# One pair of a diffusion block on TensorE: operands at one offset within 512 bytes, and another order of the last pair's fillers

## The chip, the cores and the metric

The kernel runs on one core of a Trainium2 chip. Its time is device microseconds of one execution; the number for a kernel is the median of several. TensorE does the matrix products; VectorE, ScalarE and GpSimd read and write SBUF next to it; SyncE and the other engines issue DMAs.

## The reference, cut to what matters

Two layers over 1024 latent tokens and 256 context tokens of width 1024, all in float32. The even layer projects to eight groups of 1024 channels (B, C, X, G for a gated convolution; Q, K, V, BG for neighbourhood attention of 16 heads plus the context keys), and an output projection of 2048 channels back to 1024. The odd layer is a bidirectional RG-LRU.

```python
z = u_lat @ w_in                                   # even: 1024 -> 8192
y_a = z_B * dwconv(z_C * z_X, w_conv) * silu(z_G)
y_b = neighbourhood_attention(q, k, v, k_c, v_c, rpb) * silu(z_BG)
h = h + gate * (concatenate([y_a, y_b]) @ w_out)   # 2048 -> 1024
z = u_lat @ w_in_o                                 # odd: 1024 -> 4096
x = dwconv(z[..., :2048]) + b
r, i = sigmoid(blockdiag(x, w_ra)), sigmoid(blockdiag(x, w_ri))
a = exp(8 * r * log_sigmoid(lam)); b = sqrt(1 - a*a) * i * x
y = (scan_forward(a, b) + scan_backward(a, b)) * silu(z[..., 2048:])
out = rmsnorm(h + gate * (y @ w_out_o))
```

## The kernel before

Every product is split in two parts for accuracy: an operand is kept as `hi` (rounded to the product's format) and `lo` (the rest), and each product runs three times: hi x hi, hi x lo, lo x hi. ScalarE makes `hi`, VectorE or GpSimd makes `lo`.

The even layer works in eight pairs of heads (`PAIRS`). A pair has 20 steps, one for each tile of 128 queries of a head: steps 0 to 15 have 640 keys (latent tiles), steps 16 to 19 have 256 (context tiles). In a step TensorE issues the scores of step s+1, the transposes of step s (`turn`), then filler (a projection unit of the pair, 24 products of 512 or 256 columns), then `weigh` (probabilities times V). VectorE does `row_max(s+1)`, `turn_lo(s)`, `normalise(s+1)`, then what filler asks of it, then `output(s)`. ScalarE does `turn_hi(s)`, `exp(s+1)`, the filler's copies, `copy_low(s)`.

In the last pair (`last`) there is no next pair's Q, K, V to project. `LAST_UNITS` says which units of C, X, B, G a step takes; from step 9 on, `OUT_CHUNKS` gives each step (tile, first chunk, last chunk) of the out projection's first pass: tile t is 128 tokens, its product has 16 chunks (`YC`) of 128 channels, three products of 512 columns each. What isn't done there is done in `projection()`, from tile `OUT_BEGUN` on. The weights and y have to be split first: `out_w_hi/lo(r)` for chunks 2r and 2r+1, `out_y_hi/lo(q, b, half)` for eight chunks of tile q. They are put into the steps by three functions on ScalarE and VectorE: `within(s)` is before the units' work, `ahead(s)` behind it, and `behind(s)` after `copy_low` or `output`. A second pass (`out_run`, L1652 on TensorE) does the other 512 output columns with `w1hi`, `w1lo`.

The odd layer has eight blocks, each with units X1, Z0, Z1, X0 (L2322) and four gate groups (L2341) on TensorE; then the final projection (L2351). Weight halves there are `whi` and `wlo`, of three slots; ScalarE's queue order is the order of `body`.

Buffers are laid out by hand by `Map`: the address of a tensor is `BASE` plus what stood before it; `align()` rounds up to 128 bytes.

Of the kernel before, what the change touches and what calls it, by code (L numbers as in the profile page):

```python
# [21 lines left out]
ALU = mybir.AluOpType  # L22
# [3 lines left out]
P = 128  # L26
# [11 lines left out]
YC = 16  # L38
# [40 lines left out]

class Map:  # L80
# [8 lines left out]
    def align(self):  # L89
        self.at = (self.at + P - 1) // P * P  # L90
# [77 lines left out]
LAST_UNITS = ((0,), (1,), (2, 3), (4,), (5, 6), (7, 8), (9,), (10,), (11,))  # L168


OUT_CHUNKS = {9: (0, 0, 5), 10: (0, 5, 11), 11: (0, 11, YC), 12: (1, 0, 5), 13: (1, 5, 11), 14: (1, 11, YC),
              15: (2, 0, 5), 16: (2, 5, 9), 17: (2, 9, 13), 18: (2, 13, YC), 19: (3, 0, 4)}
OUT_BEGUN = 4


def even_layer(nc, a, out, sem, k, ps, dram, uhi, ulo, ctx):
# [24 lines left out]
    m.align()  # L201
    prob_at = Map.BASE + m.at
    prob = m("probs", [P, 2, KEYS])
    pt = m("probs_t", [P, KEYS // P, 2 * P], F32R)
    low, t2 = m("pv_low", [P, 2 * P]), m("pv_out", [P, P])
    negmax, sums, rcp = m("neg_max", [P, 2]), m("row_sums", [P, 2]), m("row_rcp", [P, 2])
    small, th = m("c_cols", [P, KC, 2]), m("c_tanh", [P, KC, 2])
    ss, rms, rinv = m("sum_squares", [P, NT]), m("rms", [P, NT]), m("rms_inverse", [P, NT])
# [48 lines left out]
    ut, xn = om("u_tile", [P, KC, P]), om("xn_tile", [P, D])  # L257
# [164 lines left out]
    with nc.Block() as block:  # L422
        @block.sync
        def _(sp):
# [144 lines left out]
            def projection():  # L569
# [32 lines left out]
                load_x(0, 4, 0)  # L602
# [76 lines left out]
        def _(act):  # L679
# [232 lines left out]

            def within(s):

                if s == 7:
# [1615 lines left out]
```

## Time and profile before

| | us |
|---|---|
| median of 3 runs | 2328.14 (2328.09 to 2329.01) |
| the profiled execution | 2327.99 |
| its span | 2326.2 |
| TensorE busy in it | 2254.2 |

The span is the time from the first to the last instruction. The rows below were read from its profile. L-numbers are lines of the kernel; a name such as `ps<-u_hi,w_hi` is the tile written and the tiles read; `x24` is a count. "Idle before" is the time for which the engine stood before an instruction, and behind the arrow is who released it. A matmul's duration contains the filling and draining of the array, so products overlap: the time that one costs is the distance from its start to the next one's.

### The profile page before, as it was taken

Reading aid. Unit: us, or ns where it says so; the run is one execution under the profiler, and the core shown is the slowest. Engines: PE = TensorE matmul, PEld = TensorE weight load, DVE = VectorE, ACT = ScalarE, POOL = GpSimd, SP = SyncE. Lnnn points to the kernel's source line nnn. Section 1 sums busy time; section 2 is a strip of 40 time slices with the busy share of each in tenths; the row PEclk is TensorE's granted clock in tenths of the full one; section 3 lists DMA queues with packets and bytes.
Section 4 is the critical chain, followed back from the end, with each engine's and each line's share of the span. In section 5 each row is a group of like instructions: output and inputs, shape, how many; then the busy total and the mean of one; then the engine's idle time right before and its main releaser. Section 6 shows DMA issues by size and latency. Waiting matters only on the chain. (4 is left out here: it accounts for less than half of the span.)

```text
span 2326.2 us, 33502 instructions
## 1 busy us (share of the span) xinstructions
PE 2254.2 (97%) x11996; PEld 1910.1 (82%) x11996; DVE 1505.7 (65%) x2407; ACT 1168.1 (50%) x1696; POOL 493.5 (21%) x287
## 2 busy tenths in 40 slices
PE   6999999999999999999998999799999999999998
PEld 4788888888888888888886788688888888887787
DVE  4576575765757657577567536648667766776765
ACT  4534444345344453444434244347876787678311
POOL 0232231322323323233221030022222222220000
PEclk9999999999999999999998999899999999999999
DMA  7111221111112111122223756201111111113521
GB/s 292 37 54 52 66 61 66 54 52 62 54 59 72 52 57 59 34 70 70 66 63 121 214 168 180 85 31 55 56 54 55 55 46 64 55 55 127 208 82 64
DMA packets 146665, 187.50 MB, mean 81 GB/s; under 512 B 50520, under 2 KB 109144, under 8 KB 143448
## 3 DMA queue, kind: packets, MB, share of 16 engines
q1 hardware_dynamic: 138888, 166.67, 22.7%
q10 hardware_dynamic: 7632, 18.88, 2.2%
q8 instruction: 94, 1.54, 0.3%
q14 instruction: 51, 0.42, 0.1%
HBM read 155.62 MB, written 29.88 MB: 80 GB/s over the span
## 5 line engine op out<-in xcount | busy, mean ns | idle before, releaser
L1390 PE MATMUL ps<-u_hi,w_hi 128*128 128x512 f32 (+1 forms) x1464 | 533.2, 364 | 0.0
L1390 PE MATMUL ps<-u_hi,w_lo 128*128 128x512 f32 (+1 forms) x1464 | 519.9, 355 | 0.0
L1390 PE MATMUL ps<-u_lo,w_hi 128*128 128x512 f32 (+1 forms) x1464 | 517.8, 354 | 0.0
L1390 PEld LDWEIGHTS ps<-u_hi,w_lo 128*128 128x128 f32 x1464 | 276.4, 189 | 40.1
L1390 PEld LDWEIGHTS ps<-u_lo,w_hi 128*128 128x128 f32 x1464 | 277.1, 189 | 35.2
L1390 PEld LDWEIGHTS ps<-u_hi,w_hi 128*128 128x128 f32 x1464 | 276.5, 189 | 35.2
L2322 PE MATMUL ps<-u_hi,o_w_hi 128*128 128x512 f32 (+1 forms) x640 | 240.0, 375 | 9.4 <-POOL o_w_lo L1897 9.4
L732 ACT ACTIVATE probs<-probs,neg_max 128x640 f32<-128x640 f32 (+1 forms) x160 | 122.7, 767 | 248.5 <-DVE neg_max L1062 248.5
L1897 POOL TENSOR_TENSOR o_w_lo<-o_w_raw,o_w_hi 128x1024 fp32r<-128x1024 f32 x48 | 143.0, 2979 | 466.7 <-ACT o_w_hi L1916 466.7
L2322 PE MATMUL ps<-u_hi,o_w_lo 128*128 128x512 f32 (+1 forms) x640 | 238.7, 373 | 0.0
L2322 PE MATMUL ps<-u_lo,o_w_hi 128*128 128x512 f32 (+1 forms) x640 | 238.3, 372 | 0.0
L640 POOL TENSOR_TENSOR bias_tile<-bias_piece,col_mask 128x384 f32<-128x384 f32 x128 | 141.1, 1106 | 451.0 <-DVE neg_max L1062 450.9
L621 POOL TENSOR_TENSOR w_lo<-w_stage,w_hi 128x1024 fp32r<-128x1024 f32 x61 | 146.1, 2396 | 402.6 <-ACT w_hi L685 402.6
L1081 DVE TENSOR_TENSOR pv_low<-ps,pv_low 64x256 f32<-64x256 f32 x160 | 66.6, 416 | 237.7 <-ACT pv_low L743 236.3
L738 ACT ACTIVATE probs_t<-ps 128x640 fp32r<-128x640 f32 (+1 forms) x160 | 102.7, 642 | 105.6 <-PE ps L1414 101.8
L2322 PEld LDWEIGHTS ps<-u_hi,o_w_hi 128*128 128x128 f32 x640 | 120.8, 189 | 31.6 <-POOL o_w_lo L1897 9.8
L2322 PEld LDWEIGHTS ps<-u_hi,o_w_lo 128*128 128x128 f32 x640 | 120.8, 189 | 23.6
L2322 PEld LDWEIGHTS ps<-u_lo,o_w_hi 128*128 128x128 f32 x640 | 120.9, 189 | 22.1 <-issue 0.2
L2341 PE MATMUL ps<-x_hi,o_w_hi 128*128 128x512 f32 (+1 forms) x384 | 136.7, 356 | 1.4 <-ACT lru_r L1962 1.4
L2341 PE MATMUL ps<-x_hi,o_w_lo 128*128 128x512 f32 (+1 forms) x384 | 137.3, 358 | 0.0
L2341 PE MATMUL ps<-x_lo,o_w_hi 128*128 128x512 f32 (+1 forms) x384 | 136.9, 357 | 0.0
L1074 DVE TENSOR_TENSOR probs_t<-ps,probs_t 128x640 fp32r<-128x640 f32 (+1 forms) x160 | 118.3, 739 | 18.5 <-ACT probs_t L738 18.3
(247 smaller groups left out, 4612.8 us busy)
## 6 DMA issues: line engine op xcount, KB each, us to landing
w_stage<-in_w_even SPq DMA_DIRECT2D x63, 512.0 KB, 3.8
o_w_raw<-in_w_odd SPq DMA_DIRECT2D x48, 512.0 KB, 3.7
ada_piece<-in_w_ada SPq DMA_DIRECT2D x20, 1024.0 KB, 5.9
y_raw<-y_scratch SPq DMA_DIRECT2D x40, 512.0 KB, 6.2
wout_raw<-in_w_out SPq DMA_DIRECT2D x16, 512.0 KB, 5.9
y_scratch<-h_backward SPq DMA_DIRECT2D x16, 512.0 KB, 3.0
final_w_raw<-in_w_out SPq DMA_DIRECT2D x8, 1024.0 KB, 11.4
final_y_raw<-y_scratch SPq DMA_DIRECT2D x15, 512.0 KB, 4.6
```

What stands on the lines that cost most here:

```text
L621: nc.gpsimd.tensor_tensor(wlo[:, slot, :], stage[:, slot, :], whi[:, slot, :].bitcast(F32), ALU.subtract).then_inc(w_lo, 1)
L640: nc.gpsimd.tensor_tensor(dst, src, col, ALU.add).then_inc(t_ready, 1)
L732: nc.scalar.activation(prob[:, b, q], prob[:, b, q], ACT.Exp, scale=-1.0, bias=negmax[:, b:b + 1], accum_out=sums[:, b:b + 1]).then_inc(ex ...
L738: nc.scalar.activation(pt[:, 0:n, 0:P], turned_bank(n), ACT.Copy).then_inc(pt_hi, 1)
L1074: nc.vector.tensor_tensor(pt[:, 0:n, P:2 * P], turned_bank(n), pt[:, 0:n, 0:P].bitcast(F32), ALU.subtract).then_inc(pt_lo, 1)
L1081: nc.vector.tensor_tensor(low[r, :], ps[0:64, 6, 0:2 * P], low[r, :], ALU.add).then_inc(pv_used, 1)
L1390: last = nc.tensor.matmul(ps[:, bank(j, g), 0:t - f], w[:, slot, c * P:(c + 1) * P], x[:, c, f:t], start=(c == 0 and n == 0), stop=(c == K ...
L1897: nc.gpsimd.tensor_tensor(wlo[:, slot, :], wraw[:, slot, :], whi[:, slot, :].bitcast(F32), ALU.subtract).then_inc(w_lo, 1)
L2322: last = nc.tensor.matmul(ps[:, bank(j, g), 0:t - f], w[:, slot, c * P:(c + 1) * P], x[:, c, f:t], start=(c == 0 and q == 0), stop=(c == K ...
L2341: last = nc.tensor.matmul(ps[:, 2 + 3 * mat + g, 0:q1 - q0], w[:, slot, at:at + P], x[:, c, q0:q1], start=(c == 0 and q == 0), stop=(c == ...
```

## The change

It has two parts. First, `align()` rounds up to 512 bytes instead of 128, `ODD_RAW` is rounded down to a multiple of 512, and the x buffers of the odd layer get 1408 columns instead of 1312 (a multiple of 512 bytes); small tensors move into the gaps so made, or over others, to fit. Second, the last pair: units 9 and 10 are split in halves over steps 6 to 9, the out projection of tiles 0 and 1 is spread over steps 11 to 19 (before: of four tiles over 9 to 19), the weight and y splits are spread with it, `gate_diagonal` goes from VectorE to ScalarE and the gate rows from steps 12 and 16 to 16 and 18. In the odd layer ScalarE's `split_hi(n, GW0)` moves from the end of a block to behind `evacuate(n, X1, 1)`.

```diff
+LINE = 512
...
-        self.at = (self.at + P - 1) // P * P
+        self.at = (self.at + LINE - 1) // LINE * LINE
...
-ODD_RAW = Map.TOP - Map.BASE - 3 * KC * P * 4
+ODD_RAW = (Map.TOP - Map.BASE) // LINE * LINE - 3 * KC * P * 4
...
-LAST_UNITS = ((0,), (1,), (2, 3), (4,), (5, 6), (7, 8), (9,), (10,), (11,))
-
-
-OUT_CHUNKS = {9: (0, 0, 5), 10: (0, 5, 11), 11: (0, 11, YC), 12: (1, 0, 5), 13: (1, 5, 11), 14: (1, 11, YC),
-              15: (2, 0, 5), 16: (2, 5, 9), 17: (2, 9, 13), 18: (2, 13, YC), 19: (3, 0, 4)}
-OUT_BEGUN = 4
+LAST_UNITS = (((0, 0, 8),), ((1, 0, 8),), ((2, 0, 8), (3, 0, 8)), ((4, 0, 8),), ((5, 0, 8), (6, 0, 8)), ((7, 0, 8),),
+              ((8, 0, 8), (9, 0, 4)), ((9, 4, 8),), ((10, 0, 4),), ((10, 4, 8),), ((11, 0, 8),))
+
+
+OUT_CHUNKS = {11: (0, 0, 4), 12: (0, 4, 8), 13: (0, 8, 12), 14: (0, 12, YC), 15: (1, 0, 4), 16: (1, 4, 7), 17: (1, 7, 10),
+              18: (1, 10, 13), 19: (1, 13, YC)}
+OUT_BEGUN = 2
...
+    row_at = ada_at + 4 * 512 * 4
+    ut = over("u_tile", [P, KC, P], row_at)
+    grow = over("gate_rows", [P, 2, 2, 512], row_at + 2 * 512 * 4)
+    diag = over("gate_diag", [P, 2, 512], row_at + 6 * 512 * 4)
+    ones = over("gate_ones", [P, P], row_at + 8 * 512 * 4)
+    assert row_at + 8 * 512 * 4 + P * 4 <= x_at
...
-            return [(*ORDER[u], 0, KC) for u in LAST_UNITS[s]] if s < len(LAST_UNITS) else []
+            return [(*ORDER[u], c0, c1) for u, c0, c1 in LAST_UNITS[s]] if s < len(LAST_UNITS) else []
...
-                for t in (2, 3):
-                    for half in range(2):
-                        load_y(t, t, half)
+                for half in range(2):
+                    load_y(2, 2, half)
+                store_rest(LAT // 2, LAT, LAT_STEPS)
+                for half in range(2):
+                    load_y(3, 3, half)
                 load_x(0, 2, 0)
-                store_rest(LAT // 2, LAT, LAT_STEPS)
-                load_x(0, 3, 1)
-                sp.wait_ge(yb_stored[1], 16 * i + 16)
-                for half in range(2):
-                    load_y(4, 4, half)
                 store_rest(LAT, TOK, STEPS)
                 for stored in yb_stored:
                     sp.wait_ge(stored, 16 * PAIRS + (16 if stored is yb_stored[1] else 0))
+                for half in range(2):
+                    load_y(4, 4, half)
+                load_x(0, 3, 1)
...
+            def gate_diagonal(pass_, s):
+
+                for c in range(4):
+                    ins = nc.scalar.activation(diag[:, s, c * P:(c + 1) * P], k["ident"][:], ACT.Copy,
+                                               scale=k["modx"][:, 4 * pass_ + c, s:s + 1])
+                ins.then_inc(diag_done, 1)
+
             def within(s):
 
+                if s == 12:
+                    out_w_hi(4)
+                elif s == 13:
+                    out_w_hi(6)
+                elif s == 14:
+                    out_w_hi(7)
+
+            def ahead(s):
+
+                if s == 10:
+                    out_y_hi(0, 0, 0)
+
+            def behind(s):
+
+                i = PAIRS - 1
                 if s == 7:
-                    out_w_hi(0)
-                    out_w_hi(1)
-                elif s == 8:
-                    out_w_hi(2)
-                elif s == 9:
-                    out_w_hi(4)
-                elif s == 10:
-                    out_y_hi(0, 0, 1)
-                    out_w_hi(6)
-                elif s == 12:
-                    out_y_hi(1, 1, 1)
-
-            def ahead(s):
-
-                if s == 8:
-                    out_y_hi(0, 0, 0)
-
-            def behind(s):
-
-                i = PAIRS - 1
-                if s == 6:
                     act.wait_ge(ya_done, i + 1)
                     store_conv(act, i, 0, LAT // 2)
                 elif s == 8:
-                    out_w_hi(3)
+                    out_w_hi(0)
+                elif s == 9:
+                    out_w_hi(1)
+                elif s == 10:
+                    out_w_hi(2)
                     act.wait_ge(ya_done, i + 3)
                     store_conv(act, i, LAT // 2, LAT)
                     store_conv(act, i, LAT, TOK)
-                elif s == 9:
+                elif s == 11:
+                    out_w_hi(3)
+                    out_y_hi(0, 0, 1)
+                elif s == 12:
                     out_w_hi(5)
-                elif s == 10:
-                    out_w_hi(7)
-                elif s == 11:
+                elif s == 13:
+                    act.wait_ge(ya_stored, 32 * PAIRS + 16)
+                    gate_diagonal(0, 0)
+                elif s == 14:
                     out_y_hi(1, 1, 0)
-                elif s == 12:
+                    gate_diagonal(0, 1)
+                elif s == 15:
+                    out_y_hi(1, 1, 1)
+                elif s == 16:
                     copy_gate_row(0)
-                elif s == 13:
                     out_y_hi(2, 0, 0)
-                elif s == 14:
+                elif s == 17:
                     out_y_hi(2, 0, 1)
-                elif s == 15:
+                elif s == 18:
+                    copy_gate_row(1)
                     store_half(0)
-                elif s == 16:
-                    copy_gate_row(1)
-                    out_y_hi(3, 1, 0)
-                elif s == 17:
-                    out_y_hi(3, 1, 1)
-                    store_half(1)
...
-                for t in range(2, NT):
+                for t in range(1, NT):
                     for half in range(2):
                         out_y_hi(t + 2, t % 2, half)
                     store_half(t)
+                    if t == 3:
+                        act.wait_ge(row_mm, 2)
+                        for v in range(2):
+                            gate_diagonal(1, v)
...
             def within(s):
 
-                if s == 7:
+                if s == 12:
+                    out_w_lo(4)
+                elif s == 13:
+                    out_w_lo(6)
+                elif s == 14:
+                    out_w_lo(7)
+
+            def ahead(s):
+
+                if s == 10:
+                    out_y_lo(0, 0, 0)
+
+            def behind(s):
+
+                if s == 8:
                     out_w_lo(0)
+                elif s == 9:
                     out_w_lo(1)
-                elif s == 8:
+                elif s == 10:
                     out_w_lo(2)
-                elif s == 9:
-                    out_w_lo(4)
-                elif s == 10:
+                elif s == 11:
+                    out_w_lo(3)
                     out_y_lo(0, 0, 1)
-                    out_w_lo(6)
                 elif s == 12:
+                    out_w_lo(5)
+                elif s == 14:
+                    out_y_lo(1, 1, 0)
+                elif s == 15:
                     out_y_lo(1, 1, 1)
-                elif s == 14:
+                elif s == 16:
+                    out_y_lo(2, 0, 0)
+                elif s == 17:
+                    out_y_lo(2, 0, 1)
                     first_half(0, half_link)
-                elif s == 16:
-                    first_half(1, half_link)
-
-            def ahead(s):
-
-                if s == 8:
-                    out_y_lo(0, 0, 0)
-
-            def behind(s):
-
-                if s == 8:
-                    out_w_lo(3)
-                elif s == 9:
-                    out_w_lo(5)
-                elif s == 10:
-                    out_w_lo(7)
-                elif s == 11:
-                    out_y_lo(1, 1, 0)
-                    dve.wait_ge(ya_stored, 32 * PAIRS + 16)
-                    gate_diagonal(0, 0).then_inc(diag_done, 1)
-                elif s == 13:
-                    out_y_lo(2, 0, 0)
-                elif s == 14:
-                    out_y_lo(2, 0, 1)
-                elif s == 15:
-                    gate_diagonal(0, 1).then_inc(diag_done, 1)
-                elif s == 16:
-                    out_y_lo(3, 1, 0)
-                elif s == 17:
-                    out_y_lo(3, 1, 1)
...
-                for t in range(2, NT):
+                for t in range(1, NT):
                     first_half(t, half_link)
                     for half in range(2):
                         out_y_lo(t + 2, t % 2, half)
-                    if t == 2:
-                        dve.wait_ge(row_mm, 2)
-                        gate_diagonal(1, 0)
-                        gate_diagonal(1, 1).then_inc(diag_done, 1)
...
-                    if last and s == 12:
-                        pe.wait_ge(row_done, PAIRS)
-                        gate_row(0)
                     if last and s == 16:
                         pe.wait_ge(mod_copied, PAIRS)
+                        gate_row(0)
+                    if last and s == 18:
+                        pe.wait_ge(grow_done, 1)
                         gate_row(1)
                     if s == 14:
-                        if last:
-                            pe.wait_ge(grow_done, 1)
...
-                pe.wait_ge(diag_done, 3)
+                pe.wait_ge(diag_done, 4)
...
-                out_products(OUT_BEGUN - 1, OUT_CHUNKS[STEPS - 1][2], YC)
...
-XCOLS = 1312
+XCOLS = 1408
...
+    gaps = [X_AT + (q * XCOLS + QCOLS + 4) * 4 for q in range(3)]
+    m.at = gaps[0]
+    convw, convb, lam = m("conv_w4", [P, 64]), m("conv_b4", [P, 16]), m("lam", [P, 32])
...
-                split_hi(0, GW0)
 
             def body(n, last):
-                for g in range(1, NG):
-                    evacuate(n, X1, g)
+                evacuate(n, X1, 1)
+                split_hi(n, GW0)
+                evacuate(n, X1, 2)
...
-                    split_hi(n + 1, GW0)
```

## Rows read from the trace of the kernel before

**Rows 1.** The page, busy time of each engine, and the granted clock in 40 slices (9 is full).
```profile
PE 2254.2 (97%) x11996; PEld 1910.1 (82%) x11996; DVE 1505.7 (65%) x2407; ACT 1168.1 (50%) x1696; POOL 493.5 (21%) x287
...
PEclk9999999999999999999998999899999999999999
```

**Rows 2.** Waits of TensorE: us in total, times, longest.
```profile
PE ps L2322 <- POOL o_w_lo L1897: 9.4, 1, 9.4
PE ps L1424 <- DVE probs_t L1074: 7.2, 10, 2.3
```

**Rows 3.** Groups of instructions by form, TensorE: busy us, mean ns, idle before.
```profile
L2322 PE MATMUL ps<-u_hi,o_w_lo 128*128 128x512 f32 x512 | 202.6, 396 | 0.0
...
L1652 PE MATMUL ps<-wout_hi,u_hi 128*128 128x512 f32 x80 | 31.9, 399 | 0.0
```

**Rows 4.** The chain that ended last: start, us, what; one odd block, last stage.
```profile
1605.20 25.17 PE ps L2322 x120
1630.36 6.97 PE ps L2341 x36
...
1649.87 5.56 PE ps L2322 x24
...
1662.40 14.00 PE ps L2322 x72
...
2166.88 151.28 PE ps L2351 x666
```

**Rows 5.** Timeline of TensorE: start, us, line; two runs of products, first and next.
```profile
844.80 0.39 PE L1390 MATMUL ps<-u_hi,w_hi 128*128 128x512 f32 x1
...
850.25 0.28 PE L1406 MATMUL ps<-k_stack,q_stack 128*128 128x256 f32 x1
...
1372.02 0.40 PE L1652 MATMUL ps<-wout_hi,u_hi 128*128 128x512 f32 x1
...
1383.21 0.40 PE L1652 MATMUL ps<-wout_hi,y_hi 128*128 128x512 f32 x1
```

**Rows 6.** Windows: us, busy (instructions) of PE, PEld, DVE, ACT, POOL, granted clock, DMA.
```profile
1226.80:1233.60 6.80, 4.58 (x14) 3.44 (x14) 6.70 (x12) 3.40 (x6) 0.41 (x2) 0.50 0.84 291
1257.60:1260.90 3.30, 3.30 (x9) 2.57 (x8) 2.81 (x7) 1.88 (x3) 1.24 (x2) 0.50 0.54 159
```

**Rows 7.** Timeline of TensorE, last pair, steps 7, 10 to 12 and 19.
```profile
1212.35 0.38 PE L1414 MATMUL ps<-ident,probs 128*128 128x128 f32 x2
...
1242.83 0.50 PE L1637 MATMUL ps<-u_hi 128*128 128x512 f32 x1 [3.39 <-DVE u_lo L1150]
...
1252.86 0.77 PE L1424 MATMUL ps<-probs_t,v_stack 128*128 128x256 f32 x5
...
1254.05 0.71 PE L1414 MATMUL ps<-ident,probs 128*128 128x128 f32 x5
...
1296.54 0.41 PE L1424 MATMUL ps<-probs_t,v_stack 128*128 128x256 f32 x2
```

**Rows 8.** Timeline of VectorE, last pair, steps 7 and 10 to 12.
```profile
1222.01 0.69 DVE L1029 SCALAR_TENSOR_TENSOR conv_out<-conv_c,conv_out 128x512 f32<-128x512 f32 x1
...
1248.64 1.21 DVE L1144 TENSOR_TENSOR u_lo<-wout_raw,u_hi 128x1024 fp32r<-128x1024 f32 x1
1249.78 0.81 DVE L1062 CUSTOM_DVE_ANT_0 probs<-ps,bias_tile 128x640 f32<-128x640 f32 x1
...
1250.52 0.81 DVE L1074 TENSOR_TENSOR probs_t<-ps,probs_t 128x640 fp32r<-128x640 f32 x1
...
1251.79 0.55 DVE L1069 TENSOR_SCALAR probs<-probs,row_rcp 128x640 f32<-128x640 f32 x1
1254.08 0.42 DVE L1081 TENSOR_TENSOR pv_low<-ps,pv_low 64x256 f32<-64x256 f32 x1 [1.73 <-ACT pv_low L743]
```

**Rows 9.** Timeline of SyncE's queue and of ScalarE: load of the out weights, first split.
```profile
1211.34 2.59 SPq L522 DMA_DIRECT2D wout_raw<-in_w_out  x4
...
1217.92 2.01 ACT L889 ACTIVATE u_hi<-wout_raw 128x1024 fp32r<-128x1024 f32 x2 [1.62 <-DMA wout_raw<-in_w_out]
```

More of the change, by code:

```diff
@@ L200, in even_layer @@
     convw = m("conv_w", [P, 24])
-    m.align()
+    m.at = (m.at + P - 1) // P * P
     prob_at = Map.BASE + m.at
@@ L204, in even_layer @@
     pt = m("probs_t", [P, KEYS // P, 2 * P], F32R)
+    low_at = m.at
+    small, th = m("c_cols", [P, KC, 2]), m("c_tanh", [P, KC, 2])
+    ss, rms, rinv = m("sum_squares", [P, NT]), m("rms", [P, NT]), m("rms_inverse", [P, NT])
+    m.at = low_at
     low, t2 = m("pv_low", [P, 2 * P]), m("pv_out", [P, P])
     negmax, sums, rcp = m("neg_max", [P, 2]), m("row_sums", [P, 2]), m("row_rcp", [P, 2])
-    small, th = m("c_cols", [P, KC, 2]), m("c_tanh", [P, KC, 2])
-    ss, rms, rinv = m("sum_squares", [P, NT]), m("rms", [P, NT]), m("rms_inverse", [P, NT])
     assert Map.BASE + m.at <= Map.TOP - 2 * KC * P * 4 - SILU_BYTES
@@ L1151, in out_y_lo @@
                                         y_half(0, b, half).bitcast(F32), ALU.subtract).then_inc(y_lo, 1)
-            def gate_diagonal(pass_, s):
-                for c in range(4):
-                    ins = nc.vector.tensor_scalar(diag[:, s, c * P:(c + 1) * P], k["ident"][:],
-                                                  k["modx"][:, 4 * pass_ + c, s:s + 1], None, ALU.mult)
-                return ins
             def first_half(t, link):
@@ L1198, in behind @@
                 if s == 8:
+                    out_w_lo(0)
+                elif s == 9:
+                    out_w_lo(1)
+                elif s == 10:
+                    out_w_lo(2)
+                elif s == 11:
                     out_w_lo(3)
-                elif s == 9:
+                    out_y_lo(0, 0, 1)
+                elif s == 12:
                     out_w_lo(5)
-                elif s == 10:
-                    out_w_lo(7)
-                elif s == 11:
+                elif s == 14:
                     out_y_lo(1, 1, 0)
-                    dve.wait_ge(ya_stored, 32 * PAIRS + 16)
-                    gate_diagonal(0, 0).then_inc(diag_done, 1)
-                elif s == 13:
+                elif s == 15:
+                    out_y_lo(1, 1, 1)
+                elif s == 16:
                     out_y_lo(2, 0, 0)
-                elif s == 14:
+                elif s == 17:
                     out_y_lo(2, 0, 1)
-                elif s == 15:
-                    gate_diagonal(0, 1).then_inc(diag_done, 1)
-                elif s == 16:
-                    out_y_lo(3, 1, 0)
-                elif s == 17:
-                    out_y_lo(3, 1, 1)
+                    first_half(0, half_link)
             def out_a(pass_, t, b, i):
@@ L1690, in odd_layer @@
     m = Map(nc, PHASE)
-    convw, convb = m("conv_w4", [P, 64]), m("conv_b4", [P, 16])
-    grow, ones = m("final_gate_row", [P, D]), m("final_ones", [P, P])
-    lru, lam = m("lru_columns", [P, 5, 32]), m("lam", [P, 32])
+    grow, lru = m("final_gate_row", [P, D]), m("lru_columns", [P, 5, 32])
     bri, bra, L, Lh, nLh = (lru[:, q, :] for q in range(5))
-    own = m("lru_block_columns", [P, 5, 2, 2])
-    e_, z_, z2, den, low = (m(x, [P, 32]) for x in ("log_e", "log_z", "log_z2", "log_den", "log_low"))
     ss, var = m("final_ss", [P, NLT, 2]), m("final_var", [P, NLT])
@@ L1712, in odd_layer @@
     H0_AT = m.at
-    H0, H1 = m("h_forward", [P, 2, QCOLS]), m("h_backward", [P, 2, QCOLS])
+    H0 = m("h_forward", [P, 2, QCOLS])
+    H1_AT = m.at
+    H1 = m("h_backward", [P, 2, QCOLS])
     sg = m("silu_gate", [P, 2, LAT])
@@ L1717, in odd_layer @@
     wlo = m("o_w_lo", [P, 3, KC * P], F32R)
+    gaps = [X_AT + (q * XCOLS + QCOLS + 4) * 4 for q in range(3)]
+    m.at = gaps[0]
+    convw, convb, lam = m("conv_w4", [P, 64]), m("conv_b4", [P, 16]), m("lam", [P, 32])
+    assert m.at <= X_AT + XCOLS * 4
+    m.at = gaps[1]
+    own = m("lru_block_columns", [P, 5, 2, 2])
+    e_, z_, z2 = (m(x, [P, 32]) for x in ("log_e", "log_z", "log_z2"))
+    assert m.at <= X_AT + 2 * XCOLS * 4
+    m.at = gaps[2]
+    den, low = (m(x, [P, 32]) for x in ("log_den", "log_low"))
+    assert m.at <= X_END
     def over(name, shape, at, dt=F32):
@@ L1739, in odd_layer @@
     junk = over("final_squares", [P, 512], D * 4)
-    diag = over("final_diag", [P, KC * P], H0_AT)
+    diag, ones = over("final_diag", [P, KC * P], H0_AT), over("final_ones", [P, P], H1_AT)
     def y_raw(q):
```

18 lines of the change are left out of this document (4 added, 14 removed).

## The prediction

> **What bounds the kernel now.** I read the busy table and the slices first: TensorE is busy in 97% of the span, at its upper clock (2.4 GHz) in nearly all slices [rows 1]. The waits of TensorE come next: the two longest groups after the start are 9.4 us at the seam into the odd layer and 7.2 us in ten waits of L1424 for VectorE's `turn_lo` [rows 2]; the waits of L1637 in the last pair stand in the timeline [rows 7]. So almost every microsecond is either a matmul's period or one of few holes, and the change touches both: the periods of the odd layer and of the out projection's second pass, and the holes of the last pair.
>
> Third, the period. The chain of waits merges back-to-back matmuls, so its lines give it. One block of the odd layer repeats: 120 products of L2322 in 25.17 us, 36 of L2341 in 6.97, 24 of L2322 in 5.56, 72 in 14.00; the last stage runs 666 products of L2351 in 151.28, so 227.1 ns each [rows 4]. A 24-unit with 512 columns in 5.56 us is 231.7 ns each. The even layer, by the timeline, does 24 from 844.80 to 850.25, 227.1 ns; L1652 does 48 from 1372.02 to 1383.21, 233.1 ns [rows 5]. All are 512 columns, and the windows and slices put them all at the upper clock.
>
> I then worked out each operand's offset within 512 bytes of `Map.BASE` from the allocations. L1390 (`whi`, `wlo`, `uhi`, `ulo`): all 0; L1637: all 0; L2351: all 0. These run at 227. L1652: y at 0, `w1hi/w1lo` at 128. L2322: `whi`, `uhi`, `ulo` at 0, `wlo` at 352. L2341: `xhi` at 128 and 256, `xlo` at 384 and 0, `wlo` at 352. These run at 230 to 233. Three places alike, three unlike, no exception.
>
> **Part 1, alignment** (`LINE`, `ODD_RAW`, `XCOLS`, `align`). Price of each term if the unlike ones take 227.1 ns:
> L2322. With 512 columns: 24 x 0.2271 = 5.45 instead of 5.56, gain 0.11. The 120-line has four such units and one of 256 columns: 25.17 - 4 x 5.56 = 2.93 for the latter, which I leave; gain 0.44. The 72-line: 0.22. A block: 0.44 + 0.22 + 2 x 0.11 = 0.88 us. Eight blocks less the last one's X0 plus the prologue's X0: 7.0. I take off 0.5 for the products after each change of shape, which could need a few periods to settle. 6.5 us.
> L2341. 36 in 6.97: 24 of 512 and 12 of 260 columns. 24 x 0.2271 = 5.45 leaves 1.52 for the twelve, 127 ns each, more than the 2.93/24 = 122 ns of 256 columns; at 124 ns the line would be 6.94. Gain 0.03 of each of 32 lines, 1.0 us; bounds 0 (its 512 runs are only 12 long, too short to settle) and 2.5.
> L1652. 48 x (0.2331 - 0.2271) = 0.29 a tile, ten tiles, 2.9; less the same settling, 2.5 us.
> Sum 10.0 us, bounds 0 (the offset isn't the cause) and 12.5. All lies on the path: TensorE has no hole in the second pass and in the odd blocks. The counts agree with the list of groups: L2322 has three operand pairs of 512 products with 512 columns each, L1652 six of 80 [rows 3]. The seam's 9.4 us stays: `split_lo` and the load before it are not touched. ScalarE's `split_hi(n, GW0)` is moved back by an `evacuate` within its own queue; its user is 5 units (25 us) later, and the `evacuate` of g1 that it stood ahead of comes 1.05 us earlier: nothing either way, bound +-0.5.
>
> At this place the Trainium skill speaks against the change: "TensorE: Matmul & The Clock Gate", Part 2, step-by-step, has two independent read ports for the streaming and the stationary operand, so that loading the next weights takes no read bandwidth from the running matmul. By it the two addresses could not matter and part 1 is worth 0. The trace doesn't agree in its plain form: periods differ by 3% between stages at one clock [rows 4, 5].
>
> **Part 2, the last pair.** Before, steps 5 to 19 run with this pattern. In step 11 nothing is late [rows 7, 8]: products, `weigh` at 1252.86, next `turn` at 1254.05 (1.19 later), `output` on VectorE at 1254.08 (1.22 later), about 1.0 us with its two narrower operations; a split there takes 1.15 start to start; `row_max` at 1249.78, `turn_lo` ends 1251.33 (+1.55), normalised at 1252.34 (+2.56). Two units' gate products on VectorE cost 2 x 0.70. A chunk of out products is 3 x 0.227 = 0.68; from `turn` to its first filler I take 0.46 (its row's 0.71 less the drain of the last transpose, an estimate). Two rules follow: `weigh(s)` starts no sooner than `row_max(s+1)` + 1.6, and `turn(s+1)` no sooner than + 2.63.
> Now I place the new steps with them. Steps up to 5 lose a 256-column unit (2.9 us) and step 6 takes it: `turn(7)` at 1209.6 instead of 1212.35 [rows 7]. Then VectorE is what is late. It runs `row_max(s+1)`, `turn_lo`, normalise (2.56), the step's splits, `output` 1.0. Weigh of step 8: 1217.65; `out_w_hi(0)` then waits for its DMA: before, issue 1211.34 to ready 1217.92 [rows 9], 6.6 us; now issued at 1213.1, ready 1219.7, VectorE 1.1 late. Steps 9 and 10 carry G1 (1.4) + w1, and G2 (0.8) + y + w2: `weigh` at 1223.8 and 1229.95, with holes of 1.8 and 1.6. Steps 11 and 12, two splits each: `weigh` 1236.65 and 1243.35, holes 1.9 and 2.7 (chunk 6 of step 12 also waits for `out_w_lo(3)`, behind step 11). Step 13: 1249.45, hole 1.7 (`out_w_lo(5)`). Step 14 asks for chunks 12 to 15, and chunk 14 needs `out_w_lo(7)`, which stands inside step 14 itself behind `row_max(15)`, `turn_lo`, normalise: ready at `row_max(15)` (1252.8) + 2.56 + 0.3 for ScalarE's half + 1.15 = 1256.8, wanted at 1253.2 (two chunks behind `out_w_lo(6)`), a hole of 3.5. `weigh(14)` 1258.1, (15) 1264.3 after waiting for `out_y_lo(1,1,0)`, (16) 1268.7, (17) 1273.3, (18) 1278.6, (19) 1281.9.
> Before, `weigh(19)` starts at 1296.54 [rows 7] with 52 chunks of out products done; now 32. The 20 missing ones cost 20 x 0.68 = 13.6 us in `projection`. 1296.5 - 1281.9 - 13.6 = 1.0 us gained. Against it the clock: before, TensorE's granted clock is at 0.50 (1.2 GHz) in 1226.8 to 1233.6 and in two shorter stretches, of which one stands here [rows 6]; one follows the 3.39 us hole at 1242.83 [rows 7]; they are inside the old times. The new 3.5 us hole should bring one of the short ones: half of 3.3 us, 1.6. So part 2 is +0.6 us. Bounds: all holes gone, -10 (the walk's twelve holes, about 20 us, less what VectorE needs anyway); slow clock through steps 9 to 18, +12 (below).
> What follows is hidden: tile 2's y (splits of steps 16 and 17) is ready, tile 3's has 10.9 us (a tile: 48 x 0.227), tile 4's loads are issued after `store_rest`, about 4 us into tile 2, and needed 17 us later. `gate_diagonal` goes from VectorE to ScalarE, where eight 128-column copies meet an engine 50% busy; nothing waits but `gate_row`, two steps on. The overlaid scratch tiles cost no time.
>
> **Sum.** Profiled run 2327.99 (span 2326.2), 0.15 below the median of the runs shown. -10.0 + 0.6 = -9.4; from the median 2318.7. I say 2318.5.
>
> **Rivals.**
> A, the last pair comes out better than walked. VectorE and ScalarE queues slip past each other and the twelve holes shrink by half: 8 us of the 20, 2310.5. For it: before, ten `turn_lo` waits cost only 7.2 us in the whole run [rows 2]. Against: every step from 9 to 12 has 2.4 us or more of splits on top of 3.5 us of attention, against 4.5 us of TensorE work.
> B, the offset is not the cause (what the skill's rule says): part 1 is 0, the time is 2328.7 (2328.1 + 0.6), no change. For it: in L2322 only one operand in three pairs is unlike, and yet the whole 24-unit is slow; the odd layer could be slow through ScalarE's and VectorE's traffic. Against: L1652 is slow in a stage whose other engines do much the same as in L1637's.
> C, slower than before: the holes of steps 9 to 14 come so thick that the clock stays at 1.2 GHz from step 9 to 18. There 9 products start in 3.3 us [rows 6], where 14 fit at 0.227. TensorE's own work in steps 9 to 18 (1.75 us of attention in steps 9 to 15, about 0.8 in 16 to 18, 12 or 9 products, 24 of 256 columns and an ada row in step 10, two gate rows) is about 42 us at the upper clock, 84 at the lower; the walk gives these steps 62 us. So the full case costs 22 us: 2328.1 - 10 - 1 + 22 = 2339. It decides, that is eats part 1, from half the stretch on (11 us, 2328); three quarters, 2334, is what I name as its time. For it: five holes of 1.6 to 1.9 us and two above 2.5 in a row, where before a 3.39 us hole was enough for a drop. Against: a hole of 1.8 us between products at full rate is less idle than any that a drop followed.
> If only L1652 and half of L2322 speed up the time is 2323, within the forecast's range.
>
> **How the numbers follow.** Forecast 0.62, own range 2313 to 2324; A 0.16, B 0.13, C 0.09. Range 2308 to 2327: leaves out C, half of B, and A's far end. The measurement tells 0.2% (4.7 us) from no change: faster is the forecast, A, and a bit of B with A's steps: 0.81. Within 0.2%: most of B and weak forms of the forecast, 0.11. Slower: C with part 1 small, and B with drops: 0.08.
>
> **What would show it.** The 24-lines of L2322 at 5.46 and its 120-line near 24.7; L1652's 48 in 10.9; L2341's 36 near 6.94. A wait of L1637 for `out_w_lo(7)` of 2.2 to 3.5 us in step 14; short waits of L1424 for `turn_lo` in most of steps 8 to 18. `weigh(19)` near 1282, out pass 1 beginning within 3 us of before. Wrong is the forecast if L2322's lines stay at 5.56, or if clock 0.5 covers more than 10 us of the last pair.

## The result, and the profile after

The kernel after takes 2333.51 us (median of 12 runs, 2332.19 to 2335.17) against 2328.47 us before (12 runs, 2327.37 to 2329.48): 1.0024 of the time before, 95% interval 1.0016 to 1.0033. It is 5 us slower, and the forecast was 10 us faster, outside its range. The profiled execution took 2335.17 us, its span is 2333.4 (2326.2 before): 7.2 us to explain in the two traces.

Busy table and granted clock of the kernel after, as in [rows 1]:
```profile
PE 2247.4 (96%) x11996; PEld 1907.0 (82%) x11996; DVE 1524.5 (65%) x2391; ACT 1172.3 (50%) x1712; POOL 487.3 (21%) x287
...
PEclk9999999999999999999999999899999999999999
```
TensorE is busy for 6.8 us less and yet the kernel is longer. VectorE has fewer instructions and is busy for 18.8 us more. Its instructions got longer; that is the row to keep in mind.

The chain of waits of the kernel after answers to [rows 4]: start, us, what, and how many products. Three lines of a block, and the last stage:
```profile
1526.72 24.67 PE ps L2326 x120
1551.39 6.90 PE ps L2345 x36
1558.28 5.48 PE ps L2326 x24
...
2174.03 151.28 PE ps L2355 x666
```
L2326 is L2322 of before, L2345 is L2341. 120 products take 24.67 us instead of 25.17, 36 take 6.90 instead of 6.97, 24 take 5.48 instead of 5.56. The second pass of the output projection, as in [rows 5]; these two products are 48 apart, in 10.88 us instead of 11.19:
```profile
1374.39 0.39 PE L1646 MATMUL ps<-wout_hi,u_hi 128*128 128x512 f32 x1
...
1385.27 0.39 PE L1646 MATMUL ps<-wout_hi,y_hi 128*128 128x512 f32 x1
```
So the products are as quick as forecast. From the same timelines I cut the span at four places (start of the out projection's second pass, which is pass 1 in the code, first product of L2326, first product of the last stage, end). Everything up to pass 1 is 2.4 us longer (1374.39 against 1372.02), pass 1 and the tail up to the odd layer 2.5 us shorter (134.39 against 136.92), the odd layer 7.3 us longer (638.47 against 631.13), the last stage equal (186.1). Sum +7.2.

The waits of TensorE, as in [rows 2], show two groups that before doesn't have among its longest, with L2345 and with the conv_in of L2326:
```profile
PE ps L1420 <- DVE probs_t L1091: 11.1, 14, 1.8
PE ps L2326 <- POOL o_w_lo L1902: 9.4, 1, 9.4
PE ps L2345 <- DVE x_lo L2121: 6.7, 7, 1.2
...
PE ps L2326 <- ACT conv_in L1930: 4.0, 7, 0.6
```
Seven waits each: one in every block but one. A block, from one `columns_of` on VectorE to the next, takes 79.4 us instead of 78.2, and within it TensorE stands for 1.5 us (0.9 and 0.6, the two groups above) where it stood for 0.0. A block of the same products without a hole takes 77.05 us (e8 below), so the holes, with the overlap of products that is lost at each, cost 2.3 us a block, more than the 1.1 that the quicker products saved.

Where it comes from shows on VectorE and GpSimd in one stretch of the same block, behind the gate products of p = 3. First before: VectorE's `lru_root`, the `lru_b` that uses it, the long scan and the next block's `x_lo`, and GpSimd's `split_lo` of the next block's Z0 and GW0 weights (start, us, engine, line):
```profile
1845.37 1.50 DVE L2137 SCALAR_TENSOR_TENSOR lru_root<-lru_root,lru_r 128x1284 f32<-128x1284 f32 x1
1848.22 2.27 DVE L2142 SCALAR_TENSOR_TENSOR lru_b<-lru_b,lru_root 128x1284 f32<-128x1284 f32 x1 [1.35 <-ACT lru_root L1977]
...
1851.25 4.31 DVE L2151 TENSOR_TENSOR_SCAN h_backward<-lru_a,h_backward,lru_b 128x1024 f32<-128x1024 f32 x1
...
1861.54 3.01 DVE L2117 TENSOR_TENSOR x_lo<-x_conv,x_hi 128x1284 fp32r<-128x1284 f32 x2
...
1845.50 3.63 POOL L1897 TENSOR_TENSOR o_w_lo<-o_w_raw,o_w_hi 128x1024 fp32r<-128x1024 f32 x1 [9.89 <-ACT o_w_hi L1916]
1850.85 2.56 POOL L1897 TENSOR_TENSOR o_w_lo<-o_w_raw,o_w_hi 128x1024 fp32r<-128x1024 f32 x1 [1.72 <-ACT o_w_hi L1916]
```
The same after, and the first operation of the next block's convolution:
```profile
1848.01 3.57 DVE L2141 SCALAR_TENSOR_TENSOR lru_root<-lru_root,lru_r 128x1284 f32<-128x1284 f32 x1
1852.93 1.50 DVE L2146 SCALAR_TENSOR_TENSOR lru_b<-lru_b,lru_root 128x1284 f32<-128x1284 f32 x1 [1.34 <-ACT lru_root L1982]
...
1855.19 2.35 DVE L2155 TENSOR_TENSOR_SCAN h_backward<-lru_a,h_backward,lru_b 128x1024 f32<-128x1024 f32 x1
...
1857.93 2.63 DVE L2111 TENSOR_SCALAR x_conv<-conv_in,conv_w,conv_b 128x1284 f32<-128x1284 f32 x1 [0.33 <-ACT conv_in L1930]
...
1865.61 3.01 DVE L2121 TENSOR_TENSOR x_lo<-x_conv,x_hi 128x1284 fp32r<-128x1284 f32 x2
...
1847.70 2.52 POOL L1902 TENSOR_TENSOR o_w_lo<-o_w_raw,o_w_hi 128x1024 fp32r<-128x1024 f32 x1 [9.46 <-ACT o_w_hi L1921]
1857.48 2.39 POOL L1902 TENSOR_TENSOR o_w_lo<-o_w_raw,o_w_hi 128x1024 fp32r<-128x1024 f32 x1 [7.25 <-ACT o_w_hi L1921]
```
Before, VectorE starts 0.13 us ahead of GpSimd. It runs its 1.50 us undisturbed and GpSimd takes 1.1 us longer (3.63 against 2.52). After, GpSimd starts 0.31 us ahead and `lru_root` takes 3.57 us. Whoever starts second stands until the first is through. The Trainium skill says just that in "SBUF — State Buffer", section "Who interferes with whom": a VectorE instruction with two SBUF inputs and a GpSimd instruction that reads SBUF exclude each other for the whole instruction, and the order of issue decides who blocks. The rows agree: 2.1 us lost by the one or 1.1 by the other, in the same pair of instructions.

Before was not free of such losses either. There `lru_b` takes 0.8 us longer behind the same split (2.27 against 1.50), and the scan 2.0 us longer beside the next one (4.31 against 2.35). After, these two are gone and the first operation of the convolution is hit instead (2.63 against 0.94). From the start of `lru_root` to the end of `x_lo` VectorE takes 19.2 us before and 20.6 after, so the net loss in this stretch is 1.4 us, not 2.1.

Behind `lru_root` of p = 3 stand the square root and the `conv_in` copies on ScalarE, the scan, the next block's convolution and `x_lo`, and behind `x_lo` TensorE with the next block's gate products. Its hole there:
```profile
1789.30 0.50 PE L2345 MATMUL ps<-x_hi,o_w_hi 128*128 128x512 f32 x1 [0.90 <-DVE x_lo L2121]
```

The last pair. Granted clock in two windows, as in [rows 6], and the hole of step 14:
```profile
1257.50:1264.20 6.70, 6.70 (x27) 6.13 (x26) 3.81 (x9) 3.80 (x9) 0.00 (x0) 0.50 0.19 52
1281.40:1284.70 3.30, 3.30 (x10) 2.66 (x9) 1.19 (x4) 0.87 (x2) 0.00 (x0) 0.50 0.46 156
```
```profile
1256.01 0.50 PE L1631 MATMUL ps<-u_hi 128*128 128x512 f32 x1 [3.41 <-DVE u_lo L1161]
```
The hole is there as walked (3.5 us forecast, 3.41 found). Behind it TensorE runs at 1.2 GHz for 6.8 us, and for 3.4 us later (the granted clock is still 0.50 in 1257.5:1264.3 and 1281.4:1284.8), 10.2 us in all; before it was 13.6 us, in stretches of 6.8, 3.4 and 3.4.

### The profile page after: what moved, and what is told of

It is laid out like the page before. It is cut to its first block and busy times, and to the rows that moved or that the text cites. A ratio compares the mean times of both kernels' runs of the same rounds, so it can differ in the third digit from the quotient of the medians.

```text
span 2333.4 us, 33495 instructions
## 1 busy us (share of the span) xinstructions
PE 2247.4 (96%) x11996; PEld 1907.0 (82%) x11996; DVE 1524.5 (65%) x2391; ACT 1172.3 (50%) x1712; POOL 487.3 (21%) x287
## 5 line engine op out<-in xcount | busy, mean ns | idle before, releaser
L2326 PE MATMUL ps<-u_hi,o_w_hi 128*128 128x512 f32 (+1 forms) x640 | 238.7, 373 | 13.7 <-POOL o_w_lo L1902 9.4
L1902 POOL TENSOR_TENSOR o_w_lo<-o_w_raw,o_w_hi 128x1024 fp32r<-128x1024 f32 x48 | 137.4, 2863 | 479.9 <-ACT o_w_hi L1921 479.9
L2326 PE MATMUL ps<-u_lo,o_w_hi 128*128 128x512 f32 (+1 forms) x640 | 236.4, 369 | 0.0
L2326 PE MATMUL ps<-u_hi,o_w_lo 128*128 128x512 f32 (+1 forms) x640 | 236.4, 369 | 0.0
L2326 PEld LDWEIGHTS ps<-u_hi,o_w_hi 128*128 128x128 f32 x640 | 121.1, 189 | 37.6 <-POOL o_w_lo L1902 9.8
L2345 PE MATMUL ps<-x_hi,o_w_hi 128*128 128x512 f32 (+1 forms) x384 | 137.4, 358 | 8.1 <-DVE x_lo L2121 6.7
L2326 PEld LDWEIGHTS ps<-u_hi,o_w_lo 128*128 128x128 f32 x640 | 121.1, 189 | 20.8
L2326 PEld LDWEIGHTS ps<-u_lo,o_w_hi 128*128 128x128 f32 x640 | 121.2, 189 | 19.6 <-issue 0.2
L2345 PE MATMUL ps<-x_hi,o_w_lo 128*128 128x512 f32 (+1 forms) x384 | 136.1, 355 | 0.0
L2345 PE MATMUL ps<-x_lo,o_w_hi 128*128 128x512 f32 (+1 forms) x384 | 135.7, 353 | 0.0
L1091 DVE TENSOR_TENSOR probs_t<-ps,probs_t 128x640 fp32r<-128x640 f32 (+1 forms) x160 | 118.3, 739 | 19.4 <-ACT probs_t L745 19.2
```

The costliest lines, as they stand in the source:

```text
L1091: nc.vector.tensor_tensor(pt[:, 0:n, P:2 * P], turned_bank(n), pt[:, 0:n, 0:P].bitcast(F32), ALU.subtract).then_inc(pt_lo, 1)
L1902: nc.gpsimd.tensor_tensor(wlo[:, slot, :], wraw[:, slot, :], whi[:, slot, :].bitcast(F32), ALU.subtract).then_inc(w_lo, 1)
L2326: last = nc.tensor.matmul(ps[:, bank(j, g), 0:t - f], w[:, slot, c * P:(c + 1) * P], x[:, c, f:t], start=(c == 0 and q == 0), stop=(c == K ...
L2345: last = nc.tensor.matmul(ps[:, 2 + 3 * mat + g, 0:q1 - q0], w[:, slot, at:at + P], x[:, c, q0:q1], start=(c == 0 and q == 0), stop=(c == ...
```

## The experiments

"Before" below is the kernel before, run on the same chip with each batch (medians 2327.2 in the first, 2327.1 in the second, 2327.8 in the third).

**First batch: which part of the change costs.** Theory 1: ScalarE's moved `split_hi` of GW0 takes its cover from `x_hi`. Theory 2: the quicker products themselves.

e1, the layout alone (all edits of `LINE`, `ODD_RAW`, `XCOLS` and of the allocations; no other):
```
-        self.at = (self.at + P - 1) // P * P
+        self.at = (self.at + LINE - 1) // LINE * LINE
...
```


> The layout alone: align() to 512 bytes, ODD_RAW, XCOLS and the moved small tensors; last pair and ScalarE's order in the odd layer as before. Theory 1 (the loss in the odd layer comes from ScalarE's split_hi(n, GW0) having been moved, which moves GpSimd's split_lo beside VectorE operations on the path): the odd blocks take 77.2 to 77.4 us instead of 78.19, the second pass of the out projection 2.5 us less, in all 9 to 10 us faster, 2318.5 to 2320. Theory 2 (the quicker products themselves bring the odd layer to VectorE's and ScalarE's chain, with the same waits for x_lo and conv_in as in the changed kernel): blocks of 78.2 to 79.4, 2326 to 2334.

2330.47 us (11 runs), ratio 1.0013 (1.0004 to 1.0022).

e2, the schedule of the last pair alone (`LAST_UNITS`, `OUT_CHUNKS`, `within`, `ahead`, `behind`):


> The last pair's new order alone on the old layout. Both theories: the odd layer as before, the second pass starts 2.4 us later as in the changed kernel (1374.4 against 1372.0), so 2330.5 to 2331.5; a hole of 3.4 us before the products that wait for out_w_lo(7). Rival: the new order only pays on the new layout, then it is above 2333.

2329.76 us, ratio 1.0010 (1.0001 to 1.0019).

e3, before with the one move on ScalarE alone:
```
-                for g in range(1, NG):
-                    evacuate(n, X1, g)
+                evacuate(n, X1, 1)
+                split_hi(n, GW0)
+                evacuate(n, X1, 2)
```


> ScalarE's new place for split_hi(n, GW0) alone, old layout, old last pair. Theory 1: the first conv operation of a block stretches from 0.94 to 2.6 us here too, but the products leave it 1 us more room in a block: 2329 to 2337, and GpSimd's first split starts at the block's begin. Theory 2: no change, 2328.5.

2327.36 us, ratio 1.0003 (0.9994 to 1.0012).

e4, the kernel after with this move taken back:


> The changed kernel with split_hi(n, GW0) back at the end of the block before. Theory 1: odd blocks 77.2 to 77.4, 2320.5 to 2322.5. Theory 2: 2333 as the changed kernel.

2333.95 us, ratio 1.0026 (1.0017 to 1.0035).

Theory 1 falls twice: the move costs nothing alone, and its removal gives nothing back. What remains is the layout (+3.2 us though it makes the products of the odd blocks and of the second pass quicker) and the schedule (+2.5). In e1's trace the block is 79.4 us, with `lru_root` of p = 3 at 3.57, and TensorE stands 1.6 us a block. The wait that ends its holes is another than in the kernel after:
```profile
PE ps L2340 <- ACT conv_in L1943: 9.2, 12, 1.0
```

**Second batch: is it the collision?**

e5, e1's kernel, and VectorE makes Z0's low part itself, in the gap in which it waits for the square root:
```
-                    recur(n, 3, link)
+                    recur(n, 3, link, lambda: split_lo(n + 1, Z0))
...
-                    split_lo(chunk(n, j), (1 + j) % 3)
+                    if j not in (Z0,):
+                        split_lo(chunk(n, j), (1 + j) % 3)
```
(the first in VectorE's `body`, the second in GpSimd's; both engines also wait for the chunk ahead on `w_lo`, so that the counts keep their order.)


> Layout alone, as in e1, and one edit more in the odd blocks: the low part of the next block's Z0 weights is made by VectorE in the gap while it waits for the square root of p = 3 (1.2 us of work in a gap of 1.3), no longer by GpSimd. Theory 2a: the quicker products moved GpSimd's split of Z0 to 0.3 us before VectorE's lru_root of p = 3, the two engines shut each other out (3.57 us where it is 1.50), and the delay of 2.07 us runs through the square root, the scan, the convolution and x_lo to the gate products of the next block. Then a block falls from 79.4 to 77.3-77.9 us and the time by 7 x 1.5 to 7 x 2.1 from e1's: 2316 to 2320. Rival 2b: the aligned addresses themselves slow the odd layer (TensorE's reads against the other engines'), whatever the phase: 2330, as e1.

2317.79 us (5 runs), ratio 0.9962 (0.9949 to 0.9976): 12 us less than e1 by the ratios (0.0051 of 2327), from one instruction a block moved to another engine. The block is 77.4 us. VectorE in the stretch shown above:
```profile
1837.97 1.50 DVE L2158 SCALAR_TENSOR_TENSOR lru_root<-lru_root,lru_r 128x1284 f32<-128x1284 f32 x1
1839.38 1.22 DVE L2179 TENSOR_TENSOR o_w_lo<-o_w_raw,o_w_hi 128x1024 fp32r<-128x1024 f32 x1
1840.82 1.50 DVE L2163 SCALAR_TENSOR_TENSOR lru_b<-lru_b,lru_root 128x1284 f32<-128x1284 f32 x1 [0.21 <-ACT lru_root L1998]
...
1853.54 3.01 DVE L2138 TENSOR_TENSOR x_lo<-x_conv,x_hi 128x1284 fp32r<-128x1284 f32 x2
```
`lru_root` has its 1.50 us again, and the split's 1.22 us lie in the gap, 0.21 us of which is left (1.34 after). From `lru_root` to the end of `x_lo` it is 18.6 us where e1 has 20.7, and the block is shorter by the same 2.1 us.

e6, the same edit in the kernel before:


> The kernel before with the same edit alone (Z0's low part by VectorE in the gap). Theory 2a: its block of 78.2 us is filled by TensorE's own products, which have no hole, and its Z0 split costs VectorE only 0.77 us; so the block stays at 78.2 and the time within 1.5 us of before (2326 to 2328). A rival: VectorE's chain sets the block before as well; then the block gains up to 0.8 us and the time 5 us (2322).

2328.43 us (11 runs), ratio 1.0003 (0.9994 to 1.0012), blocks of 78.2 us. The edit is worth 12 us with quick products and nothing with slow ones. So TensorE's own products bounded the block before, and VectorE's chain, with the collision in it, bounds it after.

e7, the layout of the even layer alone: the odd layer's `align`, `ODD_RAW` and `XCOLS` as before.


> The layout of the even layer and its output projection as after, the odd layer's layout as before, the schedule as before. Theory 2: the second pass of the output projection keeps its 2.5 us and the odd layer is as before: 2324.7. Rival: the odd layer answers to any shift of the even layer, or the second pass's gain is eaten at the seam (the load and split of the first odd weights): 2327.

2324.17 us (11 runs), ratio 0.9988 (0.9979 to 0.9997): the 2.5 us of the second pass come through where the odd blocks stay at 78.2.

e8, as e5, with X1 and GW0 too:
```
                     recur(n, 2, link)
+                    split_lo(n + 1, X1)
...
+                    split_lo(n + 1, GW0)
                     columns_of(n + 1)
```


> As e5, but VectorE makes the low parts of three of the next block's weights, X1 (behind the scan of p = 2), Z0 (in the gap) and GW0 (behind the scan of p = 3), 1.2 us each, and GpSimd only the other three. Theory 2a: each of the two further splits cost VectorE 2.0 to 2.2 us of standing still beside GpSimd and now costs 1.2 us, so the tail from the last gate product to the next block's first is 1.5 us shorter than in e5 and TensorE's own 77.1 us bounds the block: 2313 to 2317. If VectorE's work itself is the limit: no better than e5.

2315.76 us (5 runs), ratio 0.9952 (0.9939 to 0.9966). The block is 77.05 us and TensorE has no hole in it. The 16 adds of `h_backward` take 1.22 us each, where they took 2.1 on average. e8 first, then the kernel after, by the same view (busy us, mean ns, idle before):
```profile
L2188 DVE TENSOR_TENSOR h_backward<-h_backward,h_forward 128x1024 f32<-128x1024 f32 x16 | 19.5, 1220 | 0.1
L1917 POOL TENSOR_TENSOR o_w_lo<-o_w_raw,o_w_hi 128x1024 fp32r<-128x1024 f32 x24 | 61.2, 2550 | 539.4 <-ACT o_w_hi L1937 539.4
```
```profile
L2164 DVE TENSOR_TENSOR h_backward<-h_backward,h_forward 128x1024 f32<-128x1024 f32 x16 | 33.7, 2105 | 0.3
L1902 POOL TENSOR_TENSOR o_w_lo<-o_w_raw,o_w_hi 128x1024 fp32r<-128x1024 f32 x48 | 137.4, 2863 | 479.9 <-ACT o_w_hi L1921 479.9
```

**Third batch: times or addresses, and the last pair.**

e9, the kernel before, with two products a block left out:
```
                     for q, (w, x) in enumerate(((whi, uhi), (whi, ulo), (wlo, uhi))):
+                        if j == X0 and g < 2 and c == 3 and q == 1:
+                            continue
```


> The kernel before, old layout, without two of the 24 x 3 products of chunk X0 in each block (one low-part product in each of its first two units, so the output is off). It does 2 x 0.232 = 0.46 us less work a block. Theory 2a (it is the time of the products that counts, not the addresses): the gate products of p = 3 and with them ScalarE's tanh, its copy of the Z0 weights and GpSimd's split come 0.46 us earlier against VectorE's chain; before, that split started 0.13 us behind lru_root of p = 3, now it starts ahead of it, lru_root takes 3.5 us instead of 1.5, and the block grows from 78.2 to 79.0-79.6: slower with less work, 2333 to 2337. Rival 2b (addresses): 8 x 0.46 faster, 2323.5.

2336.64 us (5 runs), ratio 1.0036 (1.0023 to 1.0050): less work, old addresses, and 8.9 us slower. Blocks of 79.6 us. The collision is the same one, with GpSimd 0.35 us ahead:
```profile
1848.29 3.58 DVE L2137 SCALAR_TENSOR_TENSOR lru_root<-lru_root,lru_r 128x1284 f32<-128x1284 f32 x1
...
1847.94 2.58 POOL L1897 TENSOR_TENSOR o_w_lo<-o_w_raw,o_w_hi 128x1024 fp32r<-128x1024 f32 x1 [9.42 <-ACT o_w_hi L1916]
```
This separates the two: the odd layer's loss needs no aligned address, only TensorE a little ahead.

e10, the kernel after, with weights 7 split a step earlier:
```
                 elif s == 13:
+                    out_w_hi(7)
                     act.wait_ge(ya_stored, 32 * PAIRS + 16)
-                    gate_diagonal(0, 0)
...
-                elif s == 14:
-                    out_w_lo(7)
...
+                elif s == 13:
+                    out_w_lo(7)
```
(the gate diagonal goes to ScalarE's `within(14)`.)


> The kernel after, with the last pair of output weights (7) split into high and low at the end of step 13 instead of within step 14; the first gate diagonal takes its place in step 14. Theory: the hole of 3.41 us before the output products of step 14 shrinks to 0.6, gain 2.8; if the 6.8 us at clock 0.50 that begin 1.5 us behind this hole are its doing, another 3.4: 2327 to 2328 against 2333.5. If the clock falls all the same: 2330.7. Rival: step 14 then waits for something else that is as late: 2333.

2328.57 us (11 runs), ratio to before 1.0008 (0.9998 to 1.0017), where the kernel after has 1.0024: 3.7 us less by the ratios, 4.9 by the medians. The hole and the clock:
```profile
1252.48 0.50 PE L1631 MATMUL ps<-u_hi 128*128 128x512 f32 x1 [0.64 <-DVE u_lo L1161]
```
```profile
1250.00:1285.00 35.00, 28.42 (x137) 21.95 (x138) 26.05 (x62) 18.07 (x39) 0.00 (x0) 1.00 0.31 95
```
2.8 us of hole are gone, the granted clock is 1.00 throughout, and pass 1 starts at 1368.03 instead of 1374.39, 6.4 us earlier in these two traces. Of those, 0.7 were there before the edit's place (`turn(8)`: 1212.98 against 1213.7).

e11, all that helps: the layout, three splits on VectorE as in e8, the last pair's schedule with e10's edit, ScalarE's order as before.


> The three splits on VectorE (as e8), the layout and the last pair's schedule of after with the edit of e10, and ScalarE's order of the odd blocks as before. Theory: the parts add up, so e8's 2315.8 plus what e10 stands above the schedule of before (2331.0, that is before with the layout: e1, and what its odd layer gets from VectorE's splits): 2312 if e10 comes out at 2327.5, 2316 at 2331.

2312.23 us (5 runs), ratio 0.9932 (0.9918 to 0.9945). It beats both kernels.

e12, e1's layout with `x_hi` and `x_lo` 128 bytes further on (`m.at += 128` ahead of them):


> Layout as in e1 but for x_hi and x_lo of the odd layer, which lie 128 bytes further on: weights of a gate product at 0, its columns at 128 within 512 bytes. If the offset of one operand against the other sets the period, the gate products with 512 columns have a median of 231 ns again (229 mean over the line's 512-column forms goes to 230 or more), while the projection products stay at 227. If only o_w_lo mattered, both stay at 227.

One run, 2324.24 us. The period of the gate products with 512 columns has a median of 232 ns (228 in e1, 230 before), that of the projections stays at 227. So shifting the columns of one line slows that line and not the others. Its time is a single run's, but its trace says something more: the first full block takes 80.2 us and the next ones 78.1. With slower gate products `lru_root` and the Z0 split start together in a later block (both at 1841.91), VectorE goes first at 1.50 us, and the pattern of before is kept from block to block. With that pattern and quick projections a block is 78.1 us, hardly less than the 78.2 of before, and TensorE waits 0.3 us for `x_lo` in it.

## Why the prediction was wrong

The step that failed is one sentence of part 1: "All lies on the path: TensorE has no hole in the second pass and in the odd blocks." The prices of the periods were right and their transfer to the time was not: VectorE's chain had 0.2 us of room a block where 1.0 was counted as gain, and the runs showed blocks 1.2 us longer.

- The period. Forecast 24 products in 5.46 us, 120 in about 24.7, L1652's 48 in 10.9, L2341's 36 near 6.94; found 5.48, 24.67, 10.88 and 6.90. e12 shows it for the columns of a single line. Rival B, that the offset isn't the cause, is refuted, and with it what the prediction drew from the Trainium skill, "TensorE: Matmul & The Clock Gate", Part 2, step-by-step: that the addresses could not matter. Whether the two read ports are independent, as the page has it, no run here shows.
- The second pass, -2.5 us: found -2.5, and e7 has it alone.
- The odd layer, -7.5 us (6.5 and 1.0): found +7.3. "No hole" was true of before, but I took a full TensorE for proof of slack on the other engines and looked at no row of VectorE or GpSimd in the odd blocks. There was almost none: counted from `columns_of`, `x_lo` ended at 9.06 us and the gate products that need it began at 9.27, and the pair of `lru_root` and the Z0 split stood 0.13 us from changing places. The first gate product of the block that begins at 1777.30, in the kernel before:
```profile
1786.57 0.40 PE L2341 MATMUL ps<-x_hi,o_w_hi 128*128 128x512 f32 x1
```
  The block less the stretch from `lru_root` to the end of `x_lo` is 58.8 us in e5 (77.4 less 18.6), in e1 and in the kernel after (79.4 less 20.6 or 20.7), 58.9 in e12 (78.1 less 19.2) and 59.0 before (78.2 less 19.2, with 0.2 of room). So the quick products alone, with the collisions as they stood before, would have brought a block to about 78.0 (an estimate: 58.8 and 19.2): 0.2 us of the 1.0 counted. The change of places cost 1.4 us more. With these collisions gone (e8) the block is 77.05 us, 1.14 less than before; seven such blocks are 8.0 us, and the whole odd layer is 9.5 us shorter in e8 (621.6 against 631.1, with the moved splits' own effect in it). My 7.5 was the right size only for a kernel whose VectorE has the room.
- ScalarE's moved split, 0 +-0.5: e3 and e4 show no effect.
- The last pair, +0.6 us: found +2.4 in the trace, and +2.5 in e2 by the medians (its ratio's interval: 0.2 to 4.4, which 0.6 is in). The hole of step 14 came as walked. Mis-sized was the clock: I gave it one short stretch, 1.6 us, and there were 10.2 us at 0.50 with TensorE busy throughout, which is 5.1 us. The second stretch begins 1.2 us behind a hole of 1.8 us at 1280.22, a size that the prediction argued was too small to bring one. The thin holes came smaller than walked: 1.1, 0.6, 0.8 and 1.0 us are the longest of steps 9 to 13, where I had 1.6 to 2.7. That made up for a part. How much half clock comes differs between executions of one schedule: the new one had 6.8 us of it in e2 and 13.6 in e4, the old one 10.2 to 20.4. From the first transpose of step 5 to the second pass the three traces of the new schedule take 178.1 to 180.9 us and nine of the old one 176.3 to 179.4 (median 177.0), so the size of this term is known to a microsecond or two only.
- The sign that I named for a wrong forecast, more than 10 us at clock 0.50 in the last pair, was met by 0.2 us, but the kernel before has 13.6 by the same count: it was no sign of this failure.
- `weigh(19)`: 1281.9 and 1.6 of clock make 1283.5; found 1285.3. The rest up to pass 1 came as reckoned (89.1 us against 75.5, 13.6 more; forecast 13.6).
- Rival A was half right: the thin holes of steps 9 to 13 came to about half of the 9.7 us walked, but the clock took that back.
- Rival C had the right sign for a wrong reason: its drops cover 10.2 us of the last pair, where before had 13.6 in three stretches (1226.8, 1243.9 and 1257.5), so the clock is not what makes the kernel slower than before.

No rival named what happened: a term that is right on its own engine, that another engine's chain keeps from reaching the time, and that triggers a collision between two others.

## What to carry to other kernels

When TensorE is full but one engine's chain ends exactly where it asks, a saving on TensorE is worth only what that chain allows: walk the chain once with the new times before counting the saving. In a loop, look for pairs of VectorE and GpSimd instructions on SBUF that start within a few tenths of a microsecond of each other; which one is first is decided by phase, and 2 us a block hang on it. If VectorE has a gap where it waits anyway, the small instruction is cheaper there (1.22 us) than beside it on GpSimd (2.4 us, and 2.1 us of VectorE's time); and a split that feeds TensorE goes a step ahead of its use: the hole of 3.4 us came with 10.2 us at half clock, and with the weights ready the hole was 0.6 us and the last pair had no half clock in one trace (e10) and 3.4 us in another (e11). From the first transpose of step 5 to the second pass these two take 174.1 and 175.8 us, less than any trace of the old or the new schedule.

## What the runs showed of the hardware

- Products of 128x512 take 227 to 228 ns start to start (medians) on lines whose operands all have the same offset within 512 bytes, and 230 to 233 on lines where at least one is off by 128 (e12) or 352 bytes, at the same granted clock. It is not a matter of one product's own two operands: on L2322 of before only `o_w_lo` is off, and the two products in three that don't use it take 232 and 233 ns as well. The runs don't show which port or bank does it.
- VectorE instructions whose operands are all in SBUF and GpSimd's subtraction exclude each other. Beside a running split, two-input instructions went from 1.22 to 3.25 us and from 1.50 to 3.57. With one large input it was the same: the first operation of the convolution took 2.63 instead of 0.94 (after), and even the copy of 20 columns 2.30 instead of 0.17 (e1, e11). VectorE's instructions with one operand in PSUM ran on undisturbed beside it (two at 0.64 us, before):
```profile
1788.66 1.28 DVE L2124 SCALAR_TENSOR_TENSOR silu_gate<-silu_gate,ps 128x512 f32<-128x512 f32 x2
...
1788.39 2.62 POOL L1897 TENSOR_TENSOR o_w_lo<-o_w_raw,o_w_hi 128x1024 fp32r<-128x1024 f32 x1 [13.17 <-ACT o_w_hi L1916]
```
- A loop can have two steady patterns at nearly the same product times: 78.2 us a block before and 79.6 with 0.46 us less work on TensorE (e9), 79.4 in e1 and 78.1 with gate products 4 ns slower (e12).
